# A delta-rule stage with the two heads of a pair on the two partition halves, for every chunk

## The reference

```
def step(s, xs):
    u_c, w_c, qk_c, qd_c, kt_c, gt_c = xs
    v_new = u_c - jnp.einsum('bhld,bhde->bhle', w_c, s)
    o_c = jnp.einsum('bhld,bhde->bhle', qd_c, s) + jnp.einsum('bhij,bhje->bhie', qk_c, v_new)
    s = s * gt_c[..., None, None] + jnp.einsum('bhld,bhle->bhde', kt_c, v_new)
    return s, o_c
```

## Time and profile before

| | us |
|---|---|
| median of 3 runs | 3639.25 |
| range of the runs | 3636.07 to 3640.91 |
| profiled execution, its own time | 3650.23 |
| its span in the trace | 3648.4 |
| delta stage: first memset to the last store's issue | 1723.3 to 2068.3 |
| its loop: first product with the state to the last output product | 1741.75 to 2061.7 |

### The profile page before, as it was taken

The page is one execution under the profiler, slowest core; times in us unless marked ns, Lnnn a source line. Parts: engine busy times, 40 slices in busy tenths (PEclk is TensorE's granted clock), DMA queues, the critical chain, the costliest instruction groups (busy, mean ns, idle before and its releaser), DMA issues. The chain is left out here.

```text
span 3648.4 us, 68943 instructions
## 1 busy us (share of the span) xinstructions
PE 3320.4 (91%) x26156; PEld 2830.4 (78%) x26156; DVE 2432.4 (67%) x4770; ACT 1521.8 (42%) x2959; POOL 1340.1 (37%) x1561
## 2 busy tenths in 40 slices
PE   7999999969998999998777567999996999899998
PEld 6999899958886888887777554888885888677776
DVE  7777687746987878781555454666666655656665
ACT  5555455533223323211455423666664222344443
POOL 3222222228896736400566510000000323456654
PEclk9999999979999999999899777999998999999999
DMA  5343333344436452424866344222223544222221
GB/s 156 109 116 105 102 111 108 96 149 138 139 92 199 155 173 88 136 84 121 252 226 216 78 150 166 76 88 74 74 91 122 194 155 150 101 79 78 84 99 63
DMA packets 330646, 455.19 MB, mean 125 GB/s; under 512 B 189555, under 2 KB 212371, under 8 KB 325702
## 3 DMA queue, kind: packets, MB, share of 16 engines
q1 hardware_dynamic: 330318, 450.77, 39.2%
HBM read 276.56 MB, written 176.76 MB: 124 GB/s over the span
## 5 line engine op out<-in xcount | busy, mean ns | idle before, releaser
L88 PE MATMUL b_psP<-b_w_hi,b_xT_hi 128*128 128x512 f32 x1320 | 520.0, 394 | 42.1 <-DVE b_xT_lo L1319 25.1
L89 PE MATMUL b_psP<-b_w_lo,b_xT_hi 128*128 128x512 f32 x1320 | 517.8, 392 | 0.0
L90 PE MATMUL b_psP<-b_w_hi,b_xT_lo 128*128 128x512 f32 x1320 | 517.7, 392 | 0.0
L88 PE MATMUL a_psG<-a_xT_hi,a_w_hi 128*128 128x256 f32 (+1 forms) x1536 | 454.3, 296 | 21.1 <-DVE a_xT_lo L668 19.5
L89 PE MATMUL a_psG<-a_xT_lo,a_w_hi 128*128 128x256 f32 (+1 forms) x1536 | 441.8, 288 | 0.0
L90 PE MATMUL a_psG<-a_xT_hi,a_w_lo 128*128 128x256 f32 (+1 forms) x1536 | 441.4, 287 | 0.0
L88 PE MATMUL h_psM<-h_w_hi,h_c_hi 128*128 128x512 f32 x928 | 371.7, 400 | 57.0 <-ACT h_acc L3367 20.9
L89 PE MATMUL h_psM<-h_w_lo,h_c_hi 128*128 128x512 f32 x928 | 365.7, 394 | 0.0
L90 PE MATMUL h_psM<-h_w_hi,h_c_lo 128*128 128x512 f32 x928 | 365.4, 394 | 0.0
L3534 DVE TENSOR_TENSOR h_acc<-h_acc,h_psM 128x512 f32<-128x512 f32 x322 | 210.2, 682 | 185.9 <-PE h_psM L90 146.8
L3241 POOL TENSOR_TENSOR h_c_lo<-h_c_lo_whole,h_c_hi 128x512 fp32r<-128x512 f32 x162 | 220.3, 1388 | 309.9 <-ACT h_c_hi L3341 309.9
(11 more groups left out here) (378 smaller groups left out, 7362.8 us busy)
## 6 DMA issues: line engine op xcount, KB each, us to landing
rows_b<-b_rows SPq DMA_DIRECT2D x165, 256.0 KB, 2.2
b_x_full<-xT SPq DMA_DIRECT2D x78, 512.0 KB, 4.3
qkvB<-a_act SPq DMA_DIRECT2D x16, 1536.0 KB, 5.4
d_conv_T<-qkvB SPq DMA_DIRECT2D x16, 1536.0 KB, 10.9
xT<-a_x_full SPq DMA_DIRECT2D x33, 512.0 KB, 3.4
out<-h_rows SPq DMA_DIRECT2D x33, 512.0 KB, 2.7
a_x<-in_x_prompt SPq DMA_DIRECT2D x32, 512.0 KB, 4.3
kq<-a_kq SPq DMA_DIRECT2D x128, 128.0 KB, 2.8
```

Source lines behind the costliest of these rows:

```text
L88: nc.tensor.matmul(out, x_hi, w_hi, start=first, stop=False)
L89: nc.tensor.matmul(out, x_hi, w_lo, start=False, stop=False)
L90: return nc.tensor.matmul(out, x_lo, w_hi, start=False, stop=last)
```

## The change

In the token-first tensors the two heads of a pair stand on the two partition halves for every chunk, as they do in the channel-first ones. A tensor of [128 frames, 8 heads x 64] becomes [2 heads x 64 frames, 2 chunks, 4 head pairs, 64]. All five products of a chunk then use rows e*64 of the matrix array and write partitions e*64 of PSUM, e=0,1 in turn. `psS`, `psV` and `psD` of one half x lie in one PSUM bank (two before), both heads of `psO` in one bank, with a second bank for the other chunk.

- DVE `residual`: four instructions of 128x64 in place of eight of 64x64; ACT `new_values` 128x128 in place of 64x256, `out_rows` 128x256 in place of 64x512.
- `prepare` is replaced by `turned`: eight 64x64 products with the identity, for values and keys and for each chunk, four pieces of a tile (16 PE instructions a piece). Two pieces of the next tile are turned in each chunk. `keys` is 128x256, once a chunk.
- `outputs` stands whole ahead of `new_state`; `out_sums` stands between `residual` and `state` of the odd chunk.
- Layouts in memory: `UQ`, `za` and the store go in two transfers each of 64 partitions, with pieces half as long; the columns of z_A in `w_in` and the rows of `w_out` are handed over in the new head order; `delta_sample` loads its gate and stores its output in two transfers of 256-byte pieces. `rows` is loaded in 18 transfers (9 before) and transposed in 64 instructions (32 before).

```diff
+            def turned(out, t, first, c):
+                for p in range(PAIRS):
+                    for rows_e in EVEN_ODD:
+                        last = nc.tensor.matmul(out[rows_e, p * C:(p + 1) * C],
+                                                raw(t)[rows_e, first + p, c * C:(c + 1) * C], ident[rows_e, rows_e], start=True, stop=True)
+                return last
...
-                    last = nc.tensor.matmul(psS[x][c, e, p - 2 * x, :], raw(t)[rows_e, PAIRS + p, c], old[rows_e, p, :],
+                    last = nc.tensor.matmul(psS[x][rows_e, a, :], raw(t)[rows_e, PAIRS + p, cols], old[rows_e, p, :],
...
-                    last = nc.tensor.matmul(psV[x][c, to], UQ[t % BUFS][c, e * PAIRS + p, 0, :], r[c, at], start=True, stop=True)
+                    last = nc.tensor.matmul(psV[x][rows_e, a, :], UQ[t % BUFS][rows_e, c, p, 0, :], r[c][rows_e, p, :], start=True, stop=True)
...
-                    last = nc.tensor.matmul(psD[x][rows_e, p - 2 * x, :], kt[t % 2][c, at], vn[c, at], start=True, stop=True)
+                    last = nc.tensor.matmul(psD[x][rows_e, a, :], kt[t % 2][rows_e, c, p, :], vn[c][rows_e, p, :], start=True, stop=True)
...
-                        for e in range(2):
-                            p = 2 * x + a
-                            cols = slice((2 * p + e) * C, (2 * p + e + 1) * C)
-                            h = e * PAIRS + p
-                            op = v.scalar_tensor_tensor(r[c, cols], psS[x][c, e, a, :], key_gain[c, t, h:h + 1], vt[t % 2][c, cols],
-                                                        ALU.mult, ALU.add)
+                        p = 2 * x + a
+                        op = v.scalar_tensor_tensor(r[c][:, p, :], psS[x][:, a, :], key_gain[:, n, p:p + 1], vt[t % 2][:, c, p, :],
+                                                    ALU.mult, ALU.add)
...
             for n in range(NCH):
+                ahead = n // 2 + 1
                 keys_state(n, 0)
                 keys_state(n, 1)
                 queries_state(n, 0)
+                queries_state(n, 1)
+                if ahead < NT:
+                    (turn_values, turn_keys)[n % 2](ahead, 0)
                 solved(n, 0)
-                queries_state(n, 1)
                 solved(n, 1)
                 if n:
                     outputs(n - 1, 0)
+                    outputs(n - 1, 1)
                 new_state(n, 0)
-                if n:
-                    outputs(n - 1, 1)
                 new_state(n, 1)
-                if n % 2 == 0 and n // 2 + 1 < NT:
-                    prepare(n // 2 + 1)
+                if ahead < NT:
+                    (turn_values, turn_keys)[n % 2](ahead, 1)
```

More of the change, by code:

```diff
@@ L1585, in _ @@
-            sp.dma_start(rows[H:2 * H, :], d.ssqT).then_inc(rows_in, 16)
+                for first, src in ((0, d.ketr), (2 * PAIRS, d.krow)):
+                    there = rows[first:first + PAIRS, n // 2 * 32:(n // 2 + 1) * 32].rearrange("a (c x) e i -> a c x e i", x=2)
+                    for e in range(2):
+                        sp.dma_start(there[:, :, n % 2, e, :], src[16 * n:16 * (n + 1), e * PAIRS:(e + 1) * PAIRS]
+                                     .rearrange("c a i -> a c i")).then_inc(rows_in, 16)
@@ L1586, in _ @@
+            for e in range(2):
+                sp.dma_start(rows[PAIRS:2 * PAIRS, :, e, :], d.ssqT[e * PAIRS:(e + 1) * PAIRS, :]
+                             .rearrange("a (n i) -> a n i", i=C)).then_inc(rows_in, 16)
             for t in range(BUFS):
@@ L1679, in out_rows @@
                     e.wait_ge(g_o1, t - 1)
-                e.activation(heads(o[t % 2][c, :]), psO[c, :, :, :], ACT.Copy).then_inc(s_o, 1)
+                e.activation(o[t % 2][:, n % 2, :, :], psO[n % 2], ACT.Copy).then_inc(s_o, 1)
             def out_square(t):
@@ L1747, in queries_state @@
                         pe.wait_ge(s_o, n - 1)
-                for p, e, h, at, rows_e in half_heads(x):
-                    last = nc.tensor.matmul(psO[c, e, p, :], Qd[t % 2][rows_e, p, c], old[rows_e, p, :], start=p == 0, stop=False)
+                for p, a, rows_e in half_heads(x):
+                    last = nc.tensor.matmul(psO[c][rows_e, p, :], Qd[t % 2][rows_e, p, cols], old[rows_e, p, :], start=p == 0, stop=False)
                 last.then_inc(t_qs, 1)
             def solved(n, x):
-                t, c, old = places(n)
+                t, c, cols, old = places(n)
@@ L1758, in solved @@
                 last.then_inc(t_tr, 1)
             def outputs(n, x):
-                t, c, old = places(n)
+                t, c, cols, old = places(n)
                 pe.wait_ge(s_vn, 2 * n + x + 1)
                 pe.wait_ge(t_qs, 2 * n + 2)
-                for p, e, h, at, rows_e in half_heads(x):
-                    last = nc.tensor.matmul(psO[c, e, p, :], UQ[t % BUFS][c, e * PAIRS + p, 1, :], vn[c, at], start=False, stop=p == PAIRS - 1)
+                for p, a, rows_e in half_heads(x):
+                    last = nc.tensor.matmul(psO[c][rows_e, p, :], UQ[t % BUFS][rows_e, c, p, 1, :], vn[c][rows_e, p, :],
+                                            start=False, stop=p == PAIRS - 1)
@@ L1775, in new_state @@
+                for p, a, rows_e in half_heads(x):
+                    last = nc.tensor.matmul(psD[x][rows_e, a, :], kt[t % 2][rows_e, c, p, :], vn[c][rows_e, p, :], start=True, stop=True)
                 last.then_inc(t_ds, 1)
[L1777 to L1781 removed]
+            pe.wait_ge(rows_in, 16 * (2 + NCH // 4))
@@ L1782, in _ @@
+            for n in range(NCH):
+                to = (psA, psB)[n // NT]
+                at = n % NT * 3 * PAIRS
+                last = nc.tensor.transpose(to[:, at:at + 3 * PAIRS], rows[:, n, :, :].rearrange("k e i -> k (e i)"),
+                                           ident[0:3 * PAIRS, 0:3 * PAIRS])
             last.then_inc(t_rows, 1)
             pe.wait_ge(v_scal, 2)
-            prepare(0)
+            for c in range(2):
+                turn_values(0, c)
+            for c in range(2):
+                turn_keys(0, c)
```

202 lines of the change are left out of this document (105 added, 97 removed).

## The result

The changed kernel is slower: 3660.06 us, median of five runs (3655.11 to 3664.54), beside 3639.2 us for the kernel before in the same comparison. The ratio is 1.0056, 95% interval 1.0045 to 1.0067: 21 us more, where 74 us less were forecast. The profiled execution took 3664.54 us (span 3662.7), 14.3 more than that of before.

The account below looks back on a forecast made before the run. A chain between engines, none full, bounds the kernel. At 7.05 us a tile the loop takes 237.6 us, saving 82.4; head, tail and sample stage lose 8.5: -74 us, 3565 us against the median, range 3549 to 3603.

Parts of the forecast that it names:

- The sequencer can feed that: PE in the delta loop: instructions are supplied fast enough for 26 to 29 ns a product.
- 224 x 26 to 224 x 29 ns: PE's time for a tile's 224 products with alternating halves: 5.8 to 6.5 us.
- The chain is covered: Delta loop: PE's other products just cover the waits between engines; a chunk takes PE's own 2.9 to 3.25 us.
- The copies: ACT copies of 128 columns in place of 256 between `solved` and `new_state`: 0.28 us in place of 0.38.
- Rival A: Two heads cannot write one PSUM bank at once: 58 ns a product, 13.0 us a tile, 3743 us; chance 0.10.
- Rival B: PE stays at the low clock in the loop: 50 ns a product, 11.2 us a tile, 3700 us; chance 0.03.
- Rival C: DMA binds the delta loop at 7.6 us a tile: 18 us less gain, 3583 us; chance 0.20.
- the DMA term: DMA work for a tile's 2.10 MB in the delta loop, some in shorter pieces: 6.6 to 7.6 us.
- Rival D: Chain not covered: some 0.4 us a chunk for restarts and semaphores, 7.3 us a tile, 3573; forecast with it 0.62.
- Head: Before the delta loop: more transfer issues (3.7 us), more transposes (3.6 us), first pieces at cold clock; together +6 us.
- The tail: Behind the delta loop's last state: POOL is behind by the end, +1.5 us.
- the sample stage: `delta_sample`: two more transfers in short pieces, +1 us (0 to 3).

Follow-up runs that it names:

- e_quiet: Changed kernel with only the first six tiles loaded and then used again, stores kept; 3576.72 us, loop 238.7 us.
- e_load: Changed kernel with every transfer made into buffers nothing reads, all tiles computing on the first tile's data; 3666.01 us, loop 322.2 us.
- e_paced: Changed kernel with keys and values turned by eight 128x128 transposes a tile, 4 KB and 2 KB pieces, transfers spread over a tile; 3611.76 us, ratio 0.9923.
- e_noturn: Changed kernel with keys and values turned for the first tile only, all loads kept; loop 268.2 us, gaps 61.7 us.
- e_transposes: Changed kernel with keys and values turned by eight 128x128 transposes a tile, as in the kernel before; 3616.65 us, ratio 0.9941 to the kernel before.
- e_pieces_only: Changed kernel with only `UQ` and the query decay laid out in 4 KB and 2 KB pieces again; 3653.46 us, loop 305.5 us.

## Why the prediction was wrong

- The failed step is one sentence on PE: "The sequencer can feed that: the stage behind runs 128 products in 3.70 us, 27 ns each." 128 products are one block of 256 instructions. The row shows the array's pace over instructions that were there already, and says nothing of how fast the next block comes. The window of those products in the kernel before, below, has the DMA engines full (1.18), so traffic alone doesn't slow PE; but in its trace no packet of `q8` starts between 2080 and 2118.91, behind the last of the 128. "224 x 26 to 224 x 29 ns" is the time of the array; the term that was missing is 56 blocks in place of 42, each some 5.8 us under this loop's traffic, 322 us. `e_quiet` and `e_load` show it: 238.7 and 322.2 us with the same products.

```profile
2115.00:2119.00 4.00, 4.00 (x131) 3.71 (x131) 3.77 (x5) 0.00 (x0) 0.00 (x0) 1.00 1.18 311
```

- Everything else on PE held. The array's pace was 29.2 ns, a chunk 3.27 us (forecast up to 3.25). The chain is covered; no product of PE waits above 0.5 us for DVE, ACT or POOL. The copies took 0.28 us. With the feed free the loop was 238.7 us against 237.6, and a tile took 6.96 us in the window against 7.05; that it comes so near is in part luck, since the forecast counted on the full traffic and this run has under a third of it.
- Rival A, one bank serialises, is out: 14 products that alternate between the two heads into one bank take 0.57 us (L1732, L1758, L1794), where it asked 0.9 for 16. So the rule of the Trainium skill (TensorEngine Tiling (Array Packing), "Gotcha 1: PSUM Pressure"), that row tiles cannot access one bank at the same time, does not hold here for two tiles that write different partitions. The 62 ns a matmul that the Trainium skill (TensorE: Matmul & The Clock Gate, "Wait — 56ns, not 53.3ns?") gives for hardware decode switched off are not seen: 29.2 ns. Whether it is switched off here no run shows.
- Rival B, the low clock, came in a small way and as a consequence: the granted clock was 0.90 in the window, and 1.00 in that of `e_quiet`, where PE has no long gaps.
- Rival C: the DMA term was right, 7.3 us a tile over the loop where 6.6 to 7.6 were forecast (at the loop's rate of work, 2.10 MB take 7.7). It didn't bind in the changed kernel, whose share is 0.73, since PE was slower still; in `e_paced`, with 168 products, the share is 0.93.
- Rival D, a chain that isn't covered: not seen; no wait of PE for its partners shows, and the loop without traffic has 7.46 us a tile including its start.
- Head +9.3 against +6: the issues (18 in 7.5 us, 0.42 each) and the transposes were right in size; the rows took 2.8 us longer to land behind the last issue, which the sum didn't have. The tail was +0.7 against +1.5, the sample stage -0.7 against +1.
- What sent the forecast to the wrong side was not a rival's chance but a resource that was never counted: the DMA engines were taken as a carrier of data only. The `q8` line stands on the page of before, 211 packets, and its loop has 42 blocks, one each 7.6 us, and ten "issue" gaps already.
- Left open: what a late block waits for inside the DMA engines (its own packet takes 0.9 to 1.9 us; when it was asked for isn't recorded), how mean load and bunching share in it, why `e_noturn` has more gaps than `e_transposes` at fewer instructions (its array uses a block up in 3.7 us in place of 4.3, which may be why), and the last stage's 6.5 us.

## What to carry to other kernels

Count TensorE's instructions as a transfer: products x 2 x 64 bytes, against what the engines carry meanwhile. When a change splits few large products into many small ones in a loop with the DMA share at 0.7, ask how long the array takes for a block of 128 products. Here 3.7 us was too short under that traffic, and in a quiet loop nearly long enough; in the kernel before, a block in 7.6 us of loop left 10 us of such gaps. And read a pace from a stretch longer than one block, under the traffic of the loop in question.

## What the runs showed of the hardware

- TensorE's program is fetched in packets of 16,384 bytes, 256 instructions: 211, 225, 209 and 233 packets for 168, 224, 160 and 256 products a tile.
- A late block shows as "issue" in the middle of a group of products, with 125 products or a multiple between two gaps, up to 5.6 us long in the changed kernel. PE goes on 1.2 to 1.8 us behind the landing of the packet (329 of 338 gaps). A quiet loop has a block each 4.3 us and 17.7 us of gaps, 10.3 of them in its first 26 us, while the first loads land.
- Under traffic the 16 KB packet itself takes no longer (median 1.1 us in the changed kernel and in `e_quiet`); it starts later, up to 9.5 us behind the one before it in place of 4.6.
- 64x64 products on opposite quadrants run at 29.2 ns each, into one bank or two; with 128 columns 55 ns, with 32 columns 28 ns: from 64 to 32 columns next to nothing is gained.
- Pieces of twice the size took nearly twice the time (medians: 2 KB 128 ns in the changed kernel, 4 KB 246 in `e_pieces_only`), so that a layout in larger pieces saved only 0.25 us of 7.3 a tile.
